# RWKV-7 chunk stage on Trainium2: a half's scores, masks and identities issued within the levels of the half before, and the end products regrouped

## The reference

```python
def rwkv7_scan(r, decay, k, v, kk, a):
    def step(S, inp):
        r_t, w_t, k_t, v_t, kk_t, a_t = inp
        sa = jnp.einsum('bhvk,bhk->bhv', S, -kk_t)
        S = (S * w_t[:, :, None, :]
             + sa[..., None] * (kk_t * a_t)[:, :, None, :]
             + v_t[..., None] * k_t[:, :, None, :])
        y = jnp.einsum('bhvk,bhk->bhv', S, r_t)
        return S, y
```

## Time and profile before

| | us |
|---|---|
| median of 3 runs | 2508.17 (2503.44 to 2510.92) |
| the profiled execution's own time | 2510.8 |
| its span, first to last instruction | 2509.0 |
| stretch of the eight halves, 363.67 to 668.00 | 304.33 |
| PE busy in it | 243.01 |
| DVE, ACT, POOL busy in it | 164.89, 122.17, 85.27 |

### The profile page before, as it was taken

The page is one execution under the profiler, slowest core; times in us unless marked ns, Lnnn a source line. Parts: engine busy times, 40 slices in busy tenths (PEclk is TensorE's granted clock), DMA queues, the critical chain, the costliest instruction groups (busy, mean ns, idle before and its releaser), DMA issues.

```text
span 2509.0 us, 40772 instructions
## 1 busy us (share of the span) xinstructions
PE 2292.7 (91%) x17697; PEld 1429.9 (57%) x17697; DVE 805.0 (32%) x1691; ACT 549.2 (22%) x1165; POOL 565.1 (23%) x418
## 2 busy tenths in 40 slices
PE   8999997787789999999999979989899989888987
PEld 7888776667555545888886544433334444444432
DVE  4111315663567734223232441221211111111115
ACT  4011213442466622111121320000000000000002
POOL 5333332331110013433331011111111111111110
PEclk9999998998899999999999989999999999999999
DMA  5223210003110032221225239999999999999997
GB/s 201 88 94 134 76 76 29 12 29 119 61 68 1 1 109 69 81 60 34 62 56 205 114 130 385 429 429 429 428 415 427 429 428 430 428 429 430 429 429 295
DMA packets 73945, 538.33 MB, mean 215 GB/s; under 512 B 14152, under 2 KB 16456, under 8 KB 48032
## 3 DMA queue, kind: packets, MB, share of 16 engines
q1 hardware_dynamic: 58464, 507.55, 49.4%
q0 software_dynamic: 10240, 16.82, 1.8%
q10 hardware_dynamic: 5056, 11.28, 1.5%
HBM read 502.55 MB, written 43.52 MB: 218 GB/s over the span
## 4 chain that ended last, share of the span: by engine, by line
PE 71%; DMA 16%; DVE 5%; issue 4%; ACT 3%; POOL 0%; POOLq 0%; SPq 0%; DVEq 0%; ACTq 0%
PE banks L224 44%; DMA arena<-in_wg 15%; PE banks L229 8%; PE banks L231 8%; PE banks L230 8%; PE banks L1682 2%; ACT arena L234 1%; ACT arena L1610 1%; PE banks L2968 1%; DMA arena<-in_wo 0%; DMA h2d<-arena 0%; DVE arena L1116 0%; DVE arena L3272 0%; DVE arena L1588 0%; DMA arena<-in_con 0%
## 5 line engine op out<-in xcount | busy, mean ns | idle before, releaser
L224 PE MATMUL banks<-arena 64*64 64x64 f32 (+10 forms) x14041 | 1568.3, 357 | 151.8 <-DMA arena<-in_wg 52.1
L224 PEld LDWEIGHTS banks<-arena 64*64 64x64 f32 (+2 forms) x14041 | 823.9, 153 | 824.6 <-issue 724.9
L234 ACT ACTIVATE arena<-banks 128x512 f32<-128x512 f32 (+5 forms) x357 | 194.9, 557 | 902.9 <-PE banks L224 535.8
L2962 POOL DMA_INDIRECT yb<-arena x64 | 64.8, 1012 | 789.3 <-DVE arena L3082 771.4
L3082 DVE TENSOR_SCALAR arena<-banks,arena 128x512 f32<-128x512 f32 x64 | 48.1, 751 | 502.4 <-PE banks L224 502.4
L229 PE MATMUL banks<-h1h,w2s 128*128 128x512 f32 x448 | 177.3, 396 | 1.7 <-DVE h1l L1999 1.7
L231 PE MATMUL banks<-h1h,w2s 128*128 128x512 f32 x448 | 174.7, 390 | 0.0
L230 PE MATMUL banks<-h1l,w2s 128*128 128x512 f32 x448 | 174.3, 389 | 0.0
L229 PE MATMUL banks<-hh,wlo 128*128 128x512 f32 x432 | 172.0, 398 | 0.0
L231 PE MATMUL banks<-hh,wlo 128*128 128x512 f32 x432 | 169.6, 393 | 0.0
L230 PE MATMUL banks<-hl,wlo 128*128 128x512 f32 x432 | 168.4, 390 | 0.0
(11 more groups left out here) (262 smaller groups left out, 1758.9 us busy)
## 6 DMA issues: line engine op xcount, KB each, us to landing
arena<-in_wg SPq DMA_DIRECT2D x64, 2048.0 KB, 31.1
arena<-in_wd SPq DMA_DIRECT2D x64, 2048.0 KB, 30.3
arena<-in_wu SPq DMA_DIRECT2D x63, 2048.0 KB, 26.2
arena<-in_w SPq DMA_DIRECT2D x55, 512.0 KB, 3.5
spill<-arena SPq DMA_DIRECT2D x27, 512.0 KB, 2.6
arena<-spill SPq DMA_DIRECT2D x27, 512.0 KB, 5.5
arena<-in_wo SPq DMA_DIRECT2D x16, 512.0 KB, 7.1
arena<-yb SPq DMA_DIRECT2D x8, 1024.0 KB, 12.9
```

The lines of the kernel that those rows point to most:

```text
L224: return pe.e.matmul(o, l, r, start=start, stop=stop)
L234: return act.e.activation(o, i, ACT.Copy)
L2962: return pool.e.indirect_dma_start(yb, bass.IndirectOffsetOnAxis(ap=six[:, col:col + 1].bitcast(U32), axis=0), src[:, :], None, bounds_che ...
```

## The change

- `SC` and `TTm` have two buffers (`SCs`, `TTs`); a half takes the one of its parity, the last half buffer 0. `TL`, `Fm` and `WU` stay single.
- The front of halves 1 to 6 (two score groups, AB, their three masks, the three POOL operations) is issued within levels 2, 3 and 4 of the half before, between the F and the T of the level, one part each (`pe_front`, `dve_front`, `pool_front`). Halves 0 and 7 do it at their own start (`late_front`). Half 2's front, for instance, needs the new pair's A, R, B and K within half 1.
- The transposes stand between F and T of level 0, the "end" products after T of level 0.
- POOL makes `A_first`, then `TT_first`, then `T_first`; before `T_first` came second.
- The end products go to pairs YQ (y and q, first) and HG (H and G). Within one pair ACT copies first and DVE adds after it (`Y_copied`, `H_copied`); before, ACT and DVE read different pairs. The four corners (head, chunk parity) take turns in each part.
- A half has 19 steps where it had 18, and 22 with its own front, so side steps meet other main steps.

```diff
+    def half_buffer(i, hf):
+
+        n = 2 * i + hf
+        return 0 if n == LAST_HALF else n % 2
+
+    def early_half(i, hf):
+
+        n = 2 * i + hf + 1
+        return HALVES[n] if n < LAST_HALF else None
+
+    def late_front(i, hf):
+        return 2 * i + hf in (0, LAST_HALF)
...
-        for name in ("A", "R", "B", "K"):
-            pe.wait_ge(s(name), i + 1)
         for hf in range(2):
-            n_half = 2 * i + hf
-            for g in range(2):
-                u = ps.open(pe, ("score", i, hf, g), ring="main")
-                for jj, p in CHUNKS[4 * g:4 * g + 4]:
-                    ts = tokens(hf, jj, p)
...
+            n_half, SC, TTm = 2 * i + hf, SCs[half_buffer(i, hf)], TTs[half_buffer(i, hf)]
+            ahead = early_half(i, hf)
+            if late_front(i, hf):
+                for part in range(3):
+                    pe_front(pe, i, hf, part)
                     yield
...
+                if lv == 0:
+                    pe_turned(pe, i, hf)
+                    yield
+                if lv >= 2:
+                    if ahead:
+                        pe_front(pe, *ahead, lv - 2)
+                    yield
...
+                if lv == 0:
+                    pe_ends(pe, i, hf)
+                    yield
                 if lv == 1:
...
-            uy, uq = (ps.open(pe, (key, i, hf), ring="main") for key in ("yH", "qG"))
+            u = ps.open(pe, ("YQ", i, hf), ring="main")
...
+                y, q = ([slice(512 * p + at + jj * 64, 512 * p + at + jj * 64 + 64) for p in range(2)] for at in (0, 256))
+                for h, p in CORNERS:
+                    mm(pe, u.t[H64[h], y[p]], WU[H64[p], h, jj, 64:128], SC[H64[p], h, jj, 1, :], True, False)
+                for h, p in CORNERS:
+                    mm(pe, u.t[H64[h], y[p]], TL[H64[p], jj, 3, H64[h]], SC[H64[p], h, jj, 3, :], False, True)
+                for h, p in CORNERS:
+                    t = mm(pe, u.t[H64[h], q[p]], WU[H64[p], h, jj, 0:64], SC[H64[p], h, jj, 1, :], True, True)
+            t.then_inc(u.full.sem, 1)
             yield
+            u = ps.open(pe, ("HG", i, hf), ring="main")
...
-    def wait_half(eng, i, hf):
-
-        if i or hf:
-            u = ps["yH", i, 0] if hf else ps["yH", i - 1, 1]
-            eng.wait_ge(u.full, u.v)
...
+
+            act.wait_ge(s("y_done"), i - 1)
+            u = ps["YQ", i, hf]
+            act.wait_ge(u.full, u.v)
+            copy(act, of_half(Yi[i % 2], hf), by_chunk(u, 0)).then_inc(s("Y_copied").sem, 1)
...
+            u = ps["HG", i, hf]
             act.wait_ge(u.full, u.v)
-            copy(act, of_half(Yi[i % 2], hf), by_chunk(u, 0))
-            copy(act, of_half(Hm[i % 2].rearrange("p c n -> p (c n)"), hf), by_chunk(u, 256)).then_inc(u.free.sem, 1)
+            copy(act, of_half(Hm[i % 2].rearrange("p c n -> p (c n)"), hf), by_chunk(u, 0)).then_inc(s("H_copied").sem, 1)
             yield
...
+    def dve_front(dve, i, hf, part):
+        wait_buffer(dve, i, hf)
+        if part < 2:
             sc = con[:, CON["sc"]:CON["sc"] + 256].unsqueeze(1).unsqueeze(1).to_broadcast([128, 2, 2, 256])
-            for g in range(2):
-                u = ps["score", i, hf, g]
-                dve.wait_ge(u.full, u.v)
-                dve.e.tensor_tensor(SC[:, :, 2 * g:2 * g + 2, :, :].rearrange("p h j a n -> p h j (a n)"),
-                                    u.t[:, :].rearrange("p (h j n) -> p h j n", h=2, j=2), sc, ALU.mult).then_inc(u.free.sem, 1)
-                if g == 0:
-                    yield
+            u = ps["score", i, hf, part]
+            dve.wait_ge(u.full, u.v)
+            dve.e.tensor_tensor(SCs[half_buffer(i, hf)][:, :, 2 * part:2 * part + 2, :, :].rearrange("p h j a n -> p h j (a n)"),
+                                u.t[:, :].rearrange("p (h j n) -> p h j n", h=2, j=2), sc, ALU.mult).then_inc(u.free.sem, 1)
+        else:
...
+                if lv >= 2:
+                    if ahead:
+                        dve_front(dve, *ahead, lv - 2)
+                    yield
                 evac_T(dve, dve.e.tensor_copy, i, hf, lv, 0)
...
-            u = ps["qG", i, hf]
+            u = ps["YQ", i, hf]
             dve.wait_ge(u.full, u.v)
-            dve.e.tensor_tensor(of_half(Qs[i % 2].rearrange("p c t -> p (c t)"), hf), by_chunk(u, 0),
-                                of_half(AR[i % 2][:, 1, :], hf), ALU.add)
+            dve.wait_ge(s("Y_copied"), 2 * i + hf + 1)
+            dve.e.tensor_tensor(of_half(Qs[i % 2].rearrange("p c t -> p (c t)"), hf), by_chunk(u, 256),
+                                of_half(AR[i % 2][:, 1, :], hf), ALU.add).then_inc(u.free.sem, 1)
+            yield
+            u = ps["HG", i, hf]
+            dve.wait_ge(u.full, u.v)
+            dve.wait_ge(s("H_copied"), 2 * i + hf + 1)
             dve.e.tensor_tensor(of_half(Gm[i % 2].rearrange("p c n -> p (c n)"), hf), by_chunk(u, 256),
                                 of_half(Dn[i % 2], hf), ALU.add).then_inc(u.free.sem, 1)
             yield
 
...
+    def pool_front(pool, i, hf, part):
+        SC, TTm = SCs[half_buffer(i, hf)], TTs[half_buffer(i, hf)]
+        id2 = C("id2", 0, 64).unsqueeze(1)
+        if part == 1:
+            wait_buffer(pool, i, hf)
             u = ps["score", i, hf, 1]
             pool.wait_ge(u.free, u.v)
             A = SC[:, :, :, 0, :].rearrange("p h j n -> p (h j) n")
             pool.e.tensor_tensor(A, A, id2.to_broadcast([128, 8, 64]), ALU.add).then_inc(s("A_first").sem, 1)
+            pool.wait_ge(s("A_first"), 2 * i + hf + 1)
+            pool.e.tensor_tensor(TTm[:, :, 4:8, :], SC[:, :, :, 0, :], C("m1t", 0, 64).unsqueeze(1).unsqueeze(1).to_broadcast(
+                [128, 2, 4, 64]), ALU.mult).then_inc(s("TT_first").sem, 1)
+        if part == 2:
             u = ps["AB", i, hf]
             pool.wait_ge(u.free, u.v)
             pool.e.tensor_tensor(TTm[:, :, 0:4, :], TTm[:, :, 0:4, :], id2.unsqueeze(1).to_broadcast([128, 2, 4, 64]),
                                  ALU.add).then_inc(s("T_first").sem, 1)
```

More of the change, by code:

```diff
@@ L676, in wait_main @@
         if i >= 0:
-            for name in ("yH", "qG"):
+            for name in ("YQ", "HG"):
                 u = ps[name, i, 1]
@@ L892, in mixed_up, with wait_buffer @@
         return [x for xs in itertools.zip_longest(*lists) for x in xs if x is not None]
+    HALVES = [(i, hf) for i in range(NP) for hf in range(2)]
+    LAST_HALF = 2 * NP - 1
+    def half_buffer(i, hf):
[6 more added lines that the diff above has]
+        return 2 * i + hf in (0, LAST_HALF)
+    def wait_buffer(eng, i, hf):
+        n = 2 * i + hf
+        before = n - 1 if n == LAST_HALF else n - 2
+        if before >= 0:
+            u = ps["YQ", *HALVES[before]]
+            eng.wait_ge(u.full, u.v)
     def pe_F(pe, i, hf, lv, h):
         s_, c_, _, _ = LEVELS[lv]
+        SC, TTm = SCs[half_buffer(i, hf)], TTs[half_buffer(i, hf)]
         u = ps.open(pe, ("F", i, hf, lv, h), ring="main")
@@ new lines, in pe_AB, with pe_front @@
+    def pe_AB(pe, i, hf):
+        u = ps.open(pe, ("AB", i, hf), ring="main")
+        for jj, p in CHUNKS:
+            ts = tokens(hf, jj, p)
+            for h in range(2):
+                at = 512 * h + jj * 64
+                t = mm(pe, u.t[H64[p], at:at + 64], AR[i % 2][H64[h], 0, ts], Bt[i % 2][H64[h], ts], True, True)
+        t.then_inc(u.full.sem, 1)
+    def pe_front(pe, i, hf, part):
+        if part < 2:
+            pe_score(pe, i, hf, part)
+        else:
+            pe_AB(pe, i, hf)
@@ new lines, in pe_turned, with pe_ends @@
+    def pe_turned(pe, i, hf):
+        u = ps.open(pe, ("turned", i, hf), ring="main")
+        for jj in range(4):
+            js = slice((4 * hf + jj) * 128, (4 * hf + jj + 1) * 128)
+            pe.e.transpose(u.t[:, 256 * jj:256 * jj + 128], AR[i % 2][:, 0, js], ident)
+            t = pe.e.transpose(u.t[:, 256 * jj + 128:256 * jj + 256], vq[i % 2][:, js], ident)
+        t.then_inc(u.full.sem, 1)
+    def pe_ends(pe, i, hf):
+        pe.wait_ge(s("D"), i + 1)
+        u = ps.open(pe, ("end", i, hf), ring="main")
+        for kind, left in enumerate((Bt[i % 2], Kt[i % 2])):
+            for jj in range(4):
+                for h, p in CORNERS:
+                    ts = tokens(hf, jj, p)
+                    at = 512 * h + 256 * kind + 64 * jj
+                    t = mm(pe, u.t[H64[p], at:at + 64], left[H64[h], ts], Dn[i % 2][H64[h], ts], True, True)
+        t.then_inc(u.full.sem, 1)
@@ L1122, in dve_main @@
             m1 = C("m1", 0, 64).unsqueeze(1).unsqueeze(1).to_broadcast([128, 2, 4, 64])
-            dve.e.tensor_tensor(TTm[:, :, 0:4, :], two(u)[:, :, 0:256].rearrange("p h (j n) -> p h j n", j=4), m1,
+            dve.e.tensor_tensor(TTs[half_buffer(i, hf)][:, :, 0:4, :], two(u)[:, :, 0:256].rearrange("p h (j n) -> p h j n", j=4), m1,
                                 ALU.mult).then_inc(u.free.sem, 1)
-            yield
-            yield
-            yield
+    def dve_main(dve, i):
+        for hf in range(2):
```

(10 more changed lines are left out.)

168 lines of the change are left out of this document (79 added, 89 removed).

## The result

The changed kernel takes 2531.28 us (median of 4 runs, 2530.32 to 2531.87), the kernel before 2505.81 (4 runs). The difference of the medians is 25.5 us; the ratio is 1.0096 with an interval of 1.0078 to 1.0114, which is 20 to 29 us slower. The forecast was 2507 (2492 to 2520), so the time lies above the whole range; the slower side had a chance of 0.25, and even rival B, which stood for it, ended at 2516.

What follows compares the result with a forecast made beforehand. The prediction took PE's 61 us of idle time and PE's clock as what the change can affect. Half terms summed to -9 us, the clock added 8, net -1: 2509.8 us profiled, 2507 median, range 2492 to 2520.

Steps and rivals of the forecast that it cites:

- rival B: Slower, chance 0.25: levels 2 to 4 become DVE's chain and clock drops last; +9, about 2516 us median.
- The front at the start goes: Start of halves 1 to 6: the front before F of level 0 goes, a clean gain of 8.6 us for half 3.
- The masks cost 3.1 on DVE: The next front's masks, between a level's masks and its T copy on DVE, take back 3.1 us per half.
- +5 for half 0: Half 0 keeps its front, takes half 1's masks (3.1) and has T_first 1.3 later: 5 us longer.
- The end products are nearly free: Close of each half: serial copy and add cost 0 to 0.6 us, new corner order gains 0.2, in halves 1 to 6.
- Half 2 at 35.4: Half 2, walked through with bonus waiting for rk behind POOL's front operations: 35.4 us against 34.83 before.
- Half 3 at 34.65: Half 3, walked through with WU waiting behind L1270 and L1275: 34.65 us against 38.73 before, -4.1.
- The clock, +8: PE runs at half clock after new waits at bonus and L1275 in halves 2 to 5: +8 us, bounds -5 to +12.
- Half 7, +2: Half 7 keeps its own front and has T_first last of POOL's three operations: 2 us longer.
- my -1: The forecast's net change for the profiled execution: -9 us from the halves and +8 for the clock.
- A: Faster, chance 0.33: new waits are shorter than walked and no clock charge; -15 us, 2493 us median.
- C: No change, chance 0.07: prologue and tail set the end of each half in any order; 2508 us.

Runs made afterwards that it cites:

- e8: A follow-up kernel that, unlike the changed kernel, makes none of half 1's masks in half 0; half 0 took 39.4 us there.
- the first experiment: Changed kernel with transposes and "end" products of halves 0 and 7 back in their own front; median 8.5 us below the changed kernel.
- the fastest kernel: Changed kernel plus halves 0/7 transposes and "ends" in own front, POOL front after rk, level-4 copy and odd halves' level-1 moves earlier: 2494.45 us.

## Why the prediction was wrong, point by point

- *The front at the start goes*: right. F of level 0 follows the end products; half 1 was said to be 26.2 and is 28.1.
- *The masks cost 3.1 on DVE*: in half 0 they cost nothing that the runs show (39.4 us without them in e8, 39.7 with them), so the +5 for half 0, met by +4.6, was right by luck. In the other halves they were not tested alone.
- *The end products are nearly free*: right (0.9994 for them alone).
- *Half 2 at 35.4*: measured 41.7. The place was right, the size not. F of level 1 came at 12.7 and not 9.7: a pause of 1.17 within the end products and half clock behind it, and two waits of 0.6 and 1.1 before F of level 1. From F of level 4 to bonus it took 5.7 and not 4.5 (L1232 has 2.13 beside DVE's work, I used 1.33 to 1.75). Bonus took 3.8 and not 2.1, at half clock. The 1.75 that the walk took for one operation of POOL was a mean of 1.27 and 2.24.
- *Half 3 at 34.65*: measured 41.3. Here the step itself failed: "F of level 1 at 9.5 (L820's 3.00 is now ahead of it), F of level 2 at 15.3". F of level 1 stood at 9.8, but F of level 2 at 17.9, since T of level 1 waited 3.75 (3.95 in half 5) for ACT's copy of the front's "end" products behind two table loads and a Silu; that the "end" products moved behind level 0 on ACT too was not walked. Then L1356 and L1361 took 2.16 and 2.27 and not 1.28 (1.9, behind POOL's operations; see the last section), and WU ran at half clock (1.7).
- *The clock, +8*: the term was taken for the halves together, but with it in place halves 2 to 5 still fall short by 16.7 in all. The clock at the four late waits alone measures 5.7; the rest is waits that were not in the walk.
- *Half 7, +2*: measured +6.7. The step failed: the 1.3 for `T_first` counted only the order on POOL. The transposes and "end" products had hidden the wait for it, 4.60 in the changed kernel, and it was they that moved (6.9 in the first experiment).
- *Rival B* had the sign, but its test, more than about 4 us at WU in halves 2 to 5, was not met: 3.95 and 3.94 in halves 3 and 5, 0.3 to 0.4 in halves 2 and 4. Its price, +9 over my -1, was too small: it had the masks at the lower clock as cause, where single operations in front of a copy were it. *A* and *C* fell.

The sum of my errors at full clock, half by half, is 4.7 for half 7, 24.7 for halves 2 to 5 less the 8 of the clock, 1.9 and 1.6 for halves 1 and 6, and -0.4 for half 0: together 24.5, which is the distance from the -1 of the forecast to the +23.5 measured.

## What to carry to other kernels

When a product is moved, walk its evacuation too: which engine copies it, what stands ahead of that copy there, and which later product the ring hands its banks to. Work that is moved away from a wait was its cover, and the wait has to be priced as if it were new. And a wait has its price in the clock behind it as well: in this kernel waits of 3.3 to 3.9 us cost 1.7 more in three of four places, so two orders with equal idle time are not equal.

## What the runs showed of the hardware

DVE's 128x1024 operations with two SBUF inputs and POOL's operations take turns in these traces: the one that starts second shows no progress until the other's whole operation has ended. DVE's, 1.22 to 1.28 us alone, then ends some 1.1 us after POOL's. POOL in half 3 of the changed kernel:

```profile
481.61 2.36 POOL L852 TENSOR_TENSOR arena<-arena 128x1024 f32<-128x1024 f32 x1 [14.18 <-ACT arena L771]
...
501.64 1.27 POOL L1232 TENSOR_TENSOR arena<-arena 128x512 f32<-128x512 f32 x1
...
506.38 1.26 POOL L1237 TENSOR_TENSOR arena<-arena 128x512 f32<-128x512 f32 x1
```

L852 ends at 483.97 and DVE's L822 (3.03) 1.08 later; L1232 ends at 502.91 and L1356 (2.16) 1.07 later; L1237 ends at 507.64 and L1361 (2.27) 1.09 later. With POOL idle, in half 7, L1356 and L1361 have 1.28. In the fastest kernel L822 starts 0.70 ahead of L852's end, has 1.79, and so ends 1.09 behind it. It goes the other way too: POOL's L1232 (1.27 alone) has 2.13 in half 2, where DVE's L801 was running, and ends 1.13 after it; POOL's larger L856 (2.91 instead of 2.36) ends 1.79 after L822. L1167, which reads PSUM, keeps 1.22. The Trainium skill has the interfaces to SBUF shared by the two engines, with contention where DVE has two SBUF inputs (GPSIMD Engine Reference, "1. Specifications"); the rows agree, and show the wait to be a whole operation of the other engine. The prediction took L1356 and L1361 at their unshared 1.28; L820's 3.00 and L799's 1.75 in the earlier trace rows were already durations beside POOL.

Two table loads of 1.28 us around one activation of 1.06 make it 3.6 us long for what is queued behind it.
